# Two mixers and an attention block: projections interleaved with attention units, weight slabs in pairs

## The reference

```
for l in range(2):
    mod = (silu(c) @ ada_w[l] + ada_b[l]).reshape(B, 3, 3, D)     # 9 * 1024 columns per layer
    x = x + 0.5 * gate0 * swiglu(modulate(norm(x)), ...)           # ffn (l, 0)
    x = x + gate1 * token_mix(modulate(norm(x)), ...)              # mix l
    x = x + 0.5 * gate2 * swiglu(modulate(norm(x)), ...)           # ffn (l, 1)
x = rms_norm(x)                                                    # final
# then, on 272 tokens (16 meta tokens ahead): fox attention, MoE, HGRN2, MoE

def token_mix(h, ...):
    qkv, z, b, a, q_n, kc, vc, ks, vs, kw, vw, gates = split_cols(h @ w_in, IN_SIZES)
    y_gdn = gated_deltanet(silu(causal_dwconv(qkv)), z, b, a, ...)   # 4 heads of 128
    y_nsa = native_sparse_attention(q_n, kc, ...)                    # 8 heads of 64
    return concatenate([y_gdn, y_nsa]) @ w_out

def fox_attention(h, ...):            # 16 heads of 64
    q, k, v, f_logit = split(h @ w_in)
    s = norm(q) @ norm(k).T / 8 + cum(log f)[query] - cum(log f)[key]
    return (softmax(causal(s)) @ v) @ w_out
```

## Time and profile before

| | |
|---|---|
| median of 3 runs | 3339.81 us (3338.42 to 3344.32) |
| the profiled execution, its own time | 3344.84 us |
| its span, first to last instruction | 3343.1 us |
| PE busy in it | 2922.2 us (87%) |
| DVE busy | 1452.7 us (43%) |
| ACT busy | 787.7 us (24%) |
| DMA queue q1 (slabs) | 698.93 MB, 52.5% of 16 engines |

### The profile page before, as it was taken

One profiled execution on the slowest core, in us unless ns is written; L12 is line 12 of the kernel. 1 busy time (PEld: TensorE's weight loads), 2 busy tenths in 40 slices (PEclk: granted clock), 3 DMA queues, 4 the chain that ended last, 5 costly groups with the idle time before them and its releaser, 6 DMA issues.

```text
span 3343.1 us, 43275 instructions
## 1 busy us (share of the span) xinstructions
PE 2922.2 (87%) x17606; PEld 2132.8 (64%) x17606; DVE 1452.7 (43%) x3244; ACT 787.7 (24%) x1477; POOL 0.2 (0%) x4
## 2 busy tenths in 40 slices
PE   6999776699999977679999998998988987999998
PEld 5998675599899867559987565333334675433333
DVE  3867433377676742336521313333333343233333
ACT  3331222243333122224322221101101232110100
POOL 0000000000000000000000000000000000000000
PEclk9999785699999978569999558999999997999999
DMA  8766300156466520014442002999997221799997
GB/s 318 277 232 233 117 1 26 36 210 235 188 254 251 227 101 12 15 41 153 185 148 92 1 9 114 384 420 421 421 421 300 76 102 51 315 421 421 421 421 327
DMA packets 99372, 701.77 MB, mean 210 GB/s; under 512 B 11744, under 2 KB 14176, under 8 KB 14304
## 3 DMA queue, kind: packets, MB, share of 16 engines
q1 hardware_dynamic: 99168, 698.93, 52.5%
HBM read 697.84 MB, written 1.05 MB: 209 GB/s over the span
## 4 chain that ended last, share of the span: by engine, by line
PE 42%; DMA 12%; DVE 4%; ACT 2%; issue 1%; SPq 0%; DVEq 0%; ACTq 0%
DMA ring<-slabs 12%; PE ps L1071 8%; PE ps L684 7%; PE ps L1092 4%; PE ps L1109 3%; PE ps L865 2%; PE ps L678 2%; PE ps L1282 2%; PE ps L1283 2%; PE ps L1284 2%; PE ps L1041 1%; PE ps L852 1%; PE ps L835 1%; PE ps L839 1%; PE ps L1239 1%
## 5 line engine op out<-in xcount | busy, mean ns | idle before, releaser
L1282 PE MATMUL ps<-arena_parts 128*128 128x256 f32 x2112 | 603.1, 286 | 24.1 <-DVE arena_parts L2739 24.1
L1283 PE MATMUL ps<-arena_parts 128*128 128x256 f32 x2112 | 599.1, 284 | 0.0
L1284 PE MATMUL ps<-arena_parts,ring_parts 128*128 128x256 f32 x2112 | 598.2, 283 | 0.0
L1071 PE MATMUL ps<-ring,arena 128*64 128x512 f32 x2048 | 471.6, 603 | 52.7 <-DMA ring<-slabs 47.8
L684 PE MATMUL ps<-h,ring 128*128 128x256 f32 (+1 forms) x1920 | 457.9, 400 | 19.2 <-DVE h L2383 7.6
L684 PEld LDWEIGHTS ps<-h,ring 128*128 128x128 f32 x1920 | 377.2, 198 | 88.1 <-issue 10.9
L1282 PEld LDWEIGHTS ps<-arena_parts 128*128 128x128 f32 x2112 | 403.6, 191 | 25.5 <-issue 25.3
L1284 PEld LDWEIGHTS ps<-arena_parts,ring_parts 128*128 128x128 f32 x2112 | 402.7, 191 | 0.0
L1283 PEld LDWEIGHTS ps<-arena_parts 128*128 128x128 f32 x2112 | 401.9, 190 | 0.2
L1071 PEld LDWEIGHTS ps<-ring,arena 128*64 128x64 f32 x2048 | 148.2, 138 | 302.3 <-issue 296.6
L2655 DVE TENSOR_TENSOR ring_parts<-ring,arena_parts 128x2048 fp32r<-128x2048 f32 x132 | 299.7, 2290 | 91.0 <-ACT arena_parts L1425 91.0
(11 more groups left out here) (347 smaller groups left out, 2773.7 us busy)
## 6 DMA issues: line engine op xcount, KB each, us to landing
ring<-slabs SPq DMA_DIRECT2D x662, 1024.0 KB, 13.4
constants<-const SPq DMA_DIRECT2D x1, 1372.5 KB, 7.6
x<-xT SPq DMA_DIRECT2D x1, 1024.0 KB, 9.8
outT<-x SPq DMA_DIRECT2D x1, 1024.0 KB, 4.7
vectors<-vec SPq DMA_DIRECT2D x1, 747.5 KB, 4.6
ring<-slabs SPq DMA_DIRECT2D x2, 128.0 KB, 5.5
arena<-pos SPq DMA_DIRECT2D x1, 128.0 KB, 7.4
x<-metaT SPq DMA_DIRECT2D x1, 64.0 KB, 9.8
```

Of the source, the lines that this page charges most:

```text
L1071: mm = nc.tensor.matmul(ps[W * hh:W * hh + W, e % 2, :], xe[:, e % 2, 4 * k + c], wt[:, c], start=(k == 0 and c == 0), stop=(k == 1 and c ...
L1282: nc.tensor.matmul(out, w_hi, v_hi, start=start, stop=False, skip_group_check=True)
L1283: nc.tensor.matmul(out, w_hi, v_lo, start=False, stop=False, skip_group_check=True)
L1284: return nc.tensor.matmul(out, w_lo, v_hi, start=False, stop=stop, skip_group_check=True)
```

## The change

It has four parts.

1. **Ada sums**: 16 in each of the feed-forward stages that have any (two in each of the steps 0 to 5, one in 6 to 9) instead of 12; the mixers keep 8 (mix 0) and 4 (mix 1) instead of 12 each, beside the first six slabs.
2. **Mixer order**: the sparse attention's 14 projection jobs come first, then the rope. Then each of the 16 qkv and z jobs and the two compression jobs alternates with attention units: one unit per job for units 0 to 7, two per job for units 8 to 23. The branches run selected, window, compressed. The gated delta rule comes last, and the attention's output norm and its transposes are inside its levels 0 to 2. On DVE the convolution runs per chunk, ahead of softmax_max; on ACT a job's eviction stands ahead of the exponential. The silu of qkv and z is made at the start of `gdn`. Scores and value products have one set of banks instead of two.
3. **Fox in four head groups** of 4 heads: q, k and v jobs of group g (7 jobs), then its 6 units; the jobs of the next groups, the norm's sums and the output's transposes stand behind units. Jobs use two banks instead of four. The factor 1/8 is folded into the norm's gain.
4. **MoE slabs in pairs**: two neighbouring `eup` or `edown` slabs come with one `dma_start` of 2048 KB, 16 KB per partition, once both slots are free.

```
+FFN_SHARE = 16
+MIX_ADA = ((1, 1, 2, 2, 1, 1), (1, 1, 1, 1, 0, 0))
+MIX_ORDER = (8, 9, 10, 11, 12, 13, 0, 1, 2, 3, 4, 5, 6, 7)
...
-            past = lambda n: first + min(2 * n, n + 2, ADA_PART)
+            past = lambda n: first + min(2 * n, n + FFN_SHARE - 10, FFN_SHARE)
...
+FOX_FILL = {0: ("s4", "j11"), 1: ("s5", "j12"), 2: ("s6", "j13"), 3: ("s7", "j14"), 4: ("j15",),
+            6: ("j16", "s8"), 7: ("j17", "s9"), 8: ("j18", "s10"), 9: ("j19", "s11", "t0"), 10: ("j20", "t1"), 11: ("j21",),
+            12: ("j22", "s12"), 13: ("j23", "s13"), 14: ("j24", "t2"), 15: ("j25", "s14"), 16: ("j26", "s15"),
+            17: ("j27", "t3"), 20: ("t4",), 21: ("t5",)}
...
+def paired(plan, i):
+
+    return plan[i][0] in ("eup", "edown") and plan[i + 1:i + 2] and plan[i + 1][0] in ("eup", "edown") and i % 2 == 0
...
@@ SP
+                if paired(plan, i):
+                    name, value = free[i + 1 - RING]
+                    sp.wait_ge(s[name], value)
+                    both = ap["slabs"][i:i + 2].rearrange("n p w -> (n p w)").rearrange("(p w) -> p w", p=P)
+                    sp.dma_start(ring[:, i % RING:i % RING + 2, :].rearrange("p n w -> p (n w)"), both)\
+                        .then_inc(slot_loaded[i % RING], 16)
+                    return
...
@@ PE, mixer
-                    run_jobs(q, st, 0, 30, slab, job, h_at=("h_ready", n_ready - KC))
...
+                    run_jobs(q, st, 0, 14, slab, job, h_at=("h_ready", n_ready - KC))
...
+                    for i in range(8):
+                        run_jobs(q, st, 14 + i, 15 + i, slab, job)
+                        if i == 1:
+                            await_("dve", q, "roped", 3)
+                            scores(0)
+                        elif i >= 2:
+                            piece(i - 2)
+                    await_("act", q, "kc2")
+                    for c in range(2):
+                        run_jobs(q, st, 22 + c, 23 + c, slab, job)
+                        piece(6 + c)
+                    nsa_compressed(q, st[1], job)
+                    for i in range(8):
+                        if i == 2:
+                            await_("act", q, "cmp")
+                        run_jobs(q, st, 24 + i, 25 + i, slab, job)
+                        piece(8 + 2 * i)
+                        piece(9 + 2 * i)
+                    piece(n_units)
+                    await_("dve", q, "o", n_units - 1)
                     gdn(q, st[1])
                     await_("dve", q, "y_gdn")
-                    await_("act", q, "kc2")
-                    run_jobs(q, st, 30, 32, slab, job)
-                    nsa_compressed(q, st[1])
-                    await_("act", q, "cmp")
-                    attention(q, st)
-                    turn_outputs(q, st)
...
@@ PE, fox
+                    for n_unit in range(n_units + 1):
+                        piece(n_unit)
+                        for what, i in fox_work(n_unit):
+                            if what == "j":
+                                run_jobs(q, st, i, i + 1, slab, job)
+                            elif what == "s":
+                                fox_sum(q, i)
+                            else:
+                                fox_turn(q, i)
```

More of the change, by code:

```diff
@@ L128, in nth_slab @@
 def nth_slab(st, slab, n):
-    return slab + n + (min(n, ADA_PART) if st[0] == "mix" else 0)
+    return slab + n + (sum(MIX_ADA[st[1]][:n]) if st[0] == "mix" else 0)
 def slab_width(s):
@@ L467, in _ @@
             for i in range(len(plan)):
-                load(i)
+                if not (i and paired(plan, i - 1)):
+                    load(i)
             name, value = x_written(stages)[-1]
@@ L868, in values, with piece @@
                     mark(mm, q, "pv", n)
-                scores(0)
-                for n in range(len(units) + 1):
+                def piece(n):
                     if n + 1 < len(units):
@@ L1269, in ada_cols, with mix_cols @@
                 mm.then_inc(s["ada_ps"], 1)
+            def mix_cols(q, st, lo, hi):
+                for j in range(lo, hi):
+                    ada_cols(ada_before(q) + j, j)
             def share_cols(st, step, n, m):
@@ L1918, in _ @@
                 elif st[0] == "fox":
-                    fox_act(q, job_at[q])
+                    job = job_at[q]
+                    nc.scalar.preload_act_table_set("natural_log_exp_and_others")
+                    for d in range(4):
+                        square(q, d)
                     fox_forget(q)
-                    attention(q, st)
-                    take_outputs(q, st)
+                    for d in range(3):
+                        value_in(q, job, 4 + d)
+                        root(q, d)
+                    fox_keys(q)
+                    root(q, 3)
+                    for d in range(4, 8):
+                        square(q, d)
+                    exp, copy = attention(q, st)
+                    n_units = len(attn_units(st))
+                    exp(0)
+                    for n_unit in range(n_units):
+                        copy(n_unit)
+                        if n_unit + 1 < n_units:
+                            exp(n_unit + 1)
+                        for d in FOX_SQUARE.get(n_unit, ()):
+                            square(q, d)
+                        for what, i in fox_work(n_unit):
+                            if what == "j" and stage_jobs(st)[i][0] == "fv":
+                                value_in(q, job, i)
+                            elif what == "s":
+                                root(q, i)
+                            elif what == "t":
+                                fox_output(q, i)
+                    fox_output(q, 6)
+                    fox_output(q, 7)
                 elif st[0] == "hg":
@@ new lines, in _ @@
+                        ada_col(l, 3 * ADA_PART - sum(MIX_ADA[l]), 3 * ADA_PART, ada_slabs)
+                        n_ada += 1
+                        nsa_rope(q, l)
+                        sg = view(SMALL + 128, 2, 28)
+                        await_("act", q, "sg")
+                        mark(nc.vector.tensor_scalar(sg, sg, 1.0, None, ALU.add), q, "sg1")
+                        await_("dve", q, "sg1")
+                        mark(nc.vector.reciprocal(sg, sg), q, "sg")
+                        softmax_max, output = attention(q, st)
@@ new lines, in _ @@
+                        conv(q, l, 0)
+                        conv(q, l, 1)
+                        await_("dve", q, "sg")
+                        softmax_max(0)
+                        for i in range(2, 8):
+                            conv(q, l, i)
+                            softmax_max(i - 1)
+                            if i > 2:
+                                output(i - 3)
+                        softmax_max(7)
+                        output(5)
+                        softmax_max(8)
@@ new lines, in _ @@
+                        output(6)
+                        hidden_cmp(q, 0)
+                        hidden_cmp(q, 1)
+                        for i in range(8):
+                            if i < 4:
+                                conv(q, l, 8 + i)
+                            for n_unit in (8 + 2 * i, 9 + 2 * i):
+                                if n_unit < 23:
+                                    softmax_max(n_unit + 1)
+                                output(n_unit - 1)
+                        output(23)
@@ L2786, in _ @@
+                        gdn(q, l, job)
                     elif st[0] == "hg":
```

536 lines of the change are left out of this document (302 added, 234 removed).

## The result

The changed kernel takes 3207.6 us (median of 4 runs, 3205.3 to 3211.9) against 3342.1 beside it: the ratio is 0.9596, 95% interval 0.9575 to 0.9617, 4.0% faster. The prediction said 3212, and the sum of its terms holds almost stage by stage. One of its two main reasons, that jobs cover the attention's waits, doesn't hold, as the experiments show.

The account below looks back on a forecast made before the run. The prediction saw attention bound by engine-chain waits and PE's half clock, MoE by DMA; mix 0 −42, mix 1 −49, fox −36, MoE −8, feed-forward +7 sum to −128, from 3344.8 profiled to 3212 us on the median's scale, range 3150 to 3285.

Parts of the forecast that it names:

- Attention waits, "-18" per mixer: Mixers: jobs between attention units cover PE's waits before the transposes, leaving 26 of 44.2 us, so −18 in mix 0.
- Clock in the mixers, "-15": Mixers: units mixed with jobs regain two thirds of the clock loss, −22, less +7 for jobs at half speed: −15.
- Around the attention: Mix 0: sums −3, rope −4, compression-job waits −1, output norm −5, delta rule's start +5, gate's step −1.
- Fox, "-36": Fox: small units' waits −6, clock of units 0 to 17 −29, tail −4, first group's norm +3: −36.
- MoE, "-8": MoE stages: halving the packets saves a fixed time, chosen as 5 ns per packet: −8 us.
- Feed-forward, "+7": Feed-forward stages: four more sums in each of three stages, at 0.56 us each, cost +7 us.
- rival (f): Feed-forward: steps become DVE-bound, +13, 3225 us; counted to the forecast case, which has chance 0.60.
- (a): Mixers and fox: clock is full wherever jobs are mixed in, −33 per mixer and −49 in fox, 3156; chance 0.13.
- (b): Mixers and fox: clock stays at half with attention mixed in, jobs included, +105, 3445; chance 0.05.
- (c): Mixers: waits stay, exponential behind an eviction and softmax_max behind a convolution, 44.2 us each, +36, 3248; chance 0.12.
- (d): MoE: paired slabs wait for two slots and reach PE later, +64 and the −8 gone, 3284; chance 0.05.
- (e): Mixers and fox: jobs keep full speed, units stay at half, 59 us not gained, 3271; chance 0.05.

Follow-up runs that it names:

- (6): Changed kernel with only the mixers' output of unit n back in its old place, behind the maximum of unit n+1, jobs still alternating: 3256.8 us, ratio 0.9762.
- experiment 5: Kernel before the change with only one thing added: DVE adds up each unit's output one unit later, in mixers and fox: 3244.7 us, ratio 0.9720.
- experiment 4: Changed kernel with the mixers' jobs in two lumps of eight ahead of the units instead of alternating: 3203.9 us, ratio 0.9598.
- 10: Changed kernel with the exponential ahead of the eviction, second-lot jobs behind units 8 to 15, one each, and eight smallest units alone at the end: 3154.8 us, ratio 0.9447.
- experiment 3: Changed kernel with fox's 17 jobs in lumps of seven, seven and three behind units 5, 11 and 17: 3242.9 us, ratio 0.9717.
- experiment 1: Changed kernel with its MoE slabs one by one again, 1024 KB per transfer: 3212.7 us, ratio 0.9626.
- 9: Kernel before the change with the later output, plus eight unread 272-column matmuls behind each of fox's units 8 to 23: 3263.9 us, ratio 0.9782.
- 11: Changed kernel with the mixers' exponential before the eviction, mix 0's sums beside its first four slabs, and unread matmuls behind fox's units 18 to 22: 3183.0 us, ratio 0.9533.
- (2): Changed kernel with 12 ada sums in each feed-forward stage and 12 in each mixer, two beside each of its first six slabs: 3218.0 us, ratio 0.9647.
- (7): Changed kernel with the mixers' exponential ahead of the job's eviction on ACT: 3184.0 us, ratio 0.9544.

## Why the prediction was right, and where it wasn't

**Attention waits, "-18" per mixer: the size 8 us short, the reason wrong.** The step that failed is "Units 0 to 7 get one job each, 3.58 us of work, more than the 2.11 us that they miss". The waits didn't go because jobs cover them: with jobs and the old output 36.5 us stay (6), and in the change even the units of mix 0 with a job of their own wait, 4.8 us in all. They went because DVE takes the output one unit later (5: 44.2 to 2.8 us in the kernel before, with no job near). The prediction had named the chain rightly, and had not asked which link of it the diff cuts. Then two errors met: the late output is worth 41 us of waits, and the change's own eviction in front of the exponential and its pairs of units put some 17 back (18.5 in the change, 6.2 in experiment 4, 1.8 in 10). That the net, -26, lay near the -18 of another argument is luck.

**Clock in the mixers, "-15": right.** The units' matmuls go from 71.1 to 49.7 us busy, -21 for the -22 that I took, and the jobs cost +9 for +7, so -12. But as the change has it, alternation brought nothing over lumps: in lumps (4) the clock's 10 us are lost and 12 us of waits saved. With the exponential first it pays 20 us (3184 against 3204), and with one unit per job besides 49 (3155).

**Around the attention: about right in sum.** The front is -4.9 (46.8 and 57 us for 108.9) for -3; rope and start of the delta rule take 22.0 for 23.0 us, -1, for -4 + 5 - 1; the compression jobs lie within the stretch above; the norm in the levels of the rule is -4.5 for -5. PE waits 3.42 us for the squares before the delta rule, where 5 were expected and the silu now stands in the open.

**Fox, "-36": the sum right, its first reason wrong as in the mixers.** The late output takes 11 us without any job (5). PE's wait before the transposes of all 24 units was 11.7 us; it is 1.7 in experiment 5 and 0.5 in the change, and that includes the 3.57 us at the end. The prediction had priced these waits at -6 for the small units and within -4 for the tail, as covered by other work. The clock's term, -29, is -26 in experiment 3, by the units and the jobs. The rest is some +1, where the prelude was priced at +3; it isn't taken apart further.

**MoE, "-8": 7 us, by experiment 1.** A term near zero, which the prediction names beside its own, is not what the stages show; but the 5 ns per packet were chosen, and that the two sums agree doesn't show that a fixed time per packet is the reason. hg's 2.8 us are in no term; no edit here touches that stage, and it takes 203.3 us in experiment 1, 205.7 to 206.2 in 5, 9, 10 and 11 and 208.7 in 3: what sets it isn't settled.

**Feed-forward, "+7": +9.** The place of the sums was a good trade: 10 us (2). Steps bound by DVE, rival (f), would have cost another 13 and are not to be seen.

**Rivals.** (a) falls: the clock brought -12 per mixer and -26 in fox, where it wanted -33 and -49, and the mixed stretches stand at 0.94, 0.85 and 0.89. (b) falls: the jobs lose 9 us of 57. (c), waits staying behind the eviction, was true in kind: 13 us per mixer (7). (d) falls: both MoE stages are shorter. (e) falls: the units' matmuls in the mixers are 30% shorter, and they lengthen again in lumps (3, 4). The rule of the Trainium skill (page "TensorE: Matmul & The Clock Gate", section "Why this matters for your kernels") asks that there be no idle gaps over about 3 us between bursts. The trace shows that this isn't enough: 112.0 us busy of 112.0 at 0.50 (9).

## What to carry to other kernels

When engines wait for each other in a loop, write down the ring of who waits behind whom in program order, and ask of each line of a diff whether it changes how often the ring closes; deferring one consumer by a step (with buffers for it) was worth more here than all the work that was moved into the gaps (43 us per mixer alone, for 22 and 27). When work is alternated, nothing of it may stand ahead of the critical link on any engine: the eviction, which the attention didn't need, cost 24 us (by the medians) in front of an exponential. And test a merged edit by undoing its parts singly; two parts that act on one wait don't add, and a sum that comes out right doesn't show that its terms do.

## What the runs showed of the hardware

PE's clock follows what it does and not only how busy it is: 34.00 of 34.00 and 112.0 of 112.0 us busy at 0.50 with scores, transposes and 64-column products, 0.95 with the jobs right behind them (3), 0.86 when eight matmuls of 272 columns are put behind each unit (9). Matmuls whose result nobody reads can so be paid back in large part (55 of 79 us in 9), but were never free here. Slabs in transfers of 2048 KB with 16 KB rows save about 7 us of some 1140 in the two MoE stages (1).
